# Hybrid decoder trunk: the order of work around gated linear attention (branch C)

## The chip, the cores and the metric

The kernel runs on one core of one Trainium2 chip. TensorE multiplies matrices into PSUM, VectorE, ScalarE and GpSimd do elementwise work, SyncE issues transfers, and each engine takes its own instructions in the order written and waits on semaphores for the others. The metric is the device time of one launch in microseconds (us), the median of the runs. Durations inside the kernel come from one profiled execution.

## The reference, cut to what matters

Two layers, each over 520 tokens (512 of a prompt, 8 of samples), model width 1024:

```python
z = rmsnorm(x) @ w_in                     # columns split among branches A, B, C and the gates
# A: latent attention (prompt, and samples against 4096 cached positions)
# B: spatial gating MLP
# C: gated linear attention, 4 heads, key width 64, value width 128
#    prompt: blockwise, a state per head carried along
S = exp(f)[..., None] * S + k[..., :, None] * v[..., None, :]   # samples: one step from a stored state
o = einsum('bhk,bhkv->bhv', q, S)
h_c = rmsnorm(o, g_gla) * silu(gg)        # one norm per head, over its 128 values
mix = sig(gate0) * (h_a @ w_pa) + sig(gate1) * (h_b @ w_pb) + sig(gate2) * (h_c @ w_pc)
x = x + mix @ w_o
x = x + (silu(gt) * up) @ w_down          # gt, up = rmsnorm(x) @ w_gu
```

All is float32. The kernel gets its precision by splitting each operand into a high and a low part and by three matmul passes for one product.

## The kernel before, in words

**Tiling.** Activations lie transposed, 128 channels on the partitions and 520 tokens along the row. A projection is a *group* named after its weight slab (`g03` is the fourth block of 128 columns of gate 0, `P02` the third block of `w_pa`, `wo0`, `gt0`, `up0`, `dn0` likewise). A group of `g` has 8 blocks of input channels, so 48 matmuls of 260 columns; a group of `P` has 4 and 24 matmuls. Its result takes a pair of PSUM banks, 260 columns in each.

**Weights.** ScalarE queues the load of a slab (`raw`), makes its high part (`wh`, L1223), and VectorE the low part (`wl`, L631). The helper `weights(i)` does this for every slab up to `i + 2` that isn't done yet, wherever it is called, on ScalarE and VectorE alike; TensorE waits for the low part before it starts a group. The high part of slab k waits until slab k - 3 was used.

**Banks.** `plan()` writes the groups in TensorE's order. `places()` gives each its banks, and `begin(g)` makes TensorE wait for the last reader of the group that held them before. Up to the end of the first gate stage the places are fixed or go round three pairs (the `narrow` groups, while bank 6 and 7 serve attention). After that they go round all four pairs by a counter, except some that are put on banks 6 and 7 whatever the counter says: `D0`, the even levels `L0`, `L2`, ..., `n2` and `nx`.

**Branch C's stretch.** It comes after the sample attention, whose last part is a loop of eight (`P1c`, four columns of `values`, `g1(c+1)`). The values come in pages from the cache. Then:
- `Vt0`, `Vt1`: values of branch C turned by TensorE, copied by ScalarE; `D0`, `D1`: products on the diagonal.
- seven rounds n of two levels each (`L2n`, `L2n+1`: matmuls of decayed queries and keys). VectorE collects levels 0 to 9 with `near(i)` (L1043) and makes the operands of later ones with `decayed` and `difference`; ScalarE does `decays` (exponents), and takes levels 10 to 13 with `far(i)` (L1471, L1473) and those that VectorE collected with `collected(p)` (L1480, eight copies).
- between the levels lie the gates and projections of branch A (`g00` to `g07`, `P00` to `P07`), as cover, and the samples' steps: `oh` (L1980, attention output), `Ks` (keys and values turned), `Vsel` (VectorE L1021: each sample's values on its own row, for a product), `Us` (L2013, the products k v), `sample_state` (VectorE L1033: new states), `os` (L2023, read out).
- `Kt`, `U`, `oc` (L2035, L2037): the prompt's states and outputs.
- the head norms: ScalarE squares (L1233), TensorE sums with ones (`no00` to `no11`, L1661), VectorE makes the variance (L647), ScalarE a first guess of the root (`rs_guess`, L1246), VectorE refines it in three steps (L650, L652, L654), then `y` (L1108, L1110), ScalarE the high part (`hi`, L1240), VectorE the low (`lo`, L638). `heads(p)` does this for one head after another, each with the same tiles `var`, `rs0`, `rs`.
- `merged(0, m)` (VectorE L918, L921) multiplies a gated projection and adds it; it frees the bank of `P0m`. `gate(0, m)` on ScalarE (L1387) makes the sigmoid and frees that of `g0m`.

GpSimd issues every second cache page, up to the last page of values, and sums four tiles at L2257; in this stretch it has nothing to do. Then follow the third gate stage (`g2`, `P2`), `wo`, SwiGLU (`gt`, `up`) and `dn`.

Of the kernel before, what the change touches and what calls it, by code (L numbers as in the profile page):

```python
# [14 lines left out]
GW, GH, GV = 512, 4, 128  # L15
# [199 lines left out]
def plan():  # L215
# [56 lines left out]
    for c in range(8):  # L272
        if c < 7:
            groups.append(f"pt{c + 1}n")
        if c == 2:
            groups.append("bb")
        lin(f"P1{c}")
        if c < 7:
            lin(f"g1{c + 1}")
# [5 lines left out]
    between = (["g01", "oh", "Ks0"], ["P00", "Us0"], ["g02", "Ks1", "os0"], ["P01", "Us1"], ["g03", "os1"], ["P02"], ["g04"])  # L285
# [10 lines left out]
    groups.append("oc1")  # L296
    lin("g06")
    groups.extend(["no00", "no01"])
    lin("P05", "g07")
    groups.extend(["no10", "no11"])  # L300
    lin("P06", "P07", "g20", "g21")
# [31 lines left out]
def places(groups, narrow):  # L333
# [5 lines left out]
    for g in groups:  # L339
# [44 lines left out]
def trunk(nc, a, known):  # L384
# [5 lines left out]
    with stack:  # L390
# [163 lines left out]
        assert cursor[0] <= after_ring + 16384  # L554
        Salls = [sb("Sall0", [128, 5, 128])]
# [63 lines left out]
        def _(dve):  # L619
# [83 lines left out]
            for l in range(DEPTH):  # L703
# [258 lines left out]
                for c in range(8):  # L962
# [27 lines left out]
                    if c < 7:  # L990
                        weights(si[f"g1{c + 1}"])
# [21 lines left out]

                def sample_keys(p):
                    dve.wait_ge(*upto(f"pe Ks{p}"))
                    if p:
                        dve.wait_ge(*upto("pe Us0"))
                    dve.tensor_copy(kvs[:, :, :].rearrange("p a b -> p (a b)"), bank(f"Ks{p}")[0:8, 0:384]).then_inc(*mark("dve_evac", f"free Ks{p}"))
                    dve.wait_ge(*upto(f"free Ks{p}"))
                    for e in range(2):  # L1020
                        ins = dve.tensor_tensor(Vsel[:, e, :, :],  # L1021
                                                kvs[:, 1 + e, :].unsqueeze(1).broadcast_to([8, 8, 128]),
                                                ident[0:8, 0:8].unsqueeze(2).broadcast_to([8, 8, 128]), ALU.mult)
                    ins.then_inc(*mark("value_ready", f"Vsel {p}"))
# [30 lines left out]
                weights(si["g00"])  # L1055
                evac("Ot", OT[:, :, :].rearrange("p a b -> p (a b)"), bank("Ot")[:, 0:256])
                for n in range(7):
# [7 lines left out]
                    if n == 0:  # L1065
                        weights(si["g01"])
                        sample_output()
                        sample_keys(0)
# [3 lines left out]
                    elif n == 2:  # L1072
                        weights(si["g02"])
                        sample_keys(1)
# [3 lines left out]
                    elif n == 4:  # L1078
                        for p in range(2):
                            ins = dve.memset(ATs[p][:, :, :, :], 0.0)  # L1080
                        ins.then_inc(*mark("value_ready", "AT empty"))
# [21 lines left out]
                def heads(p):  # L1103
                    for e in range(2):
                        rsqrt(f"no{p}{e}", GV, 1e-6)
                        y = ynext()
                        dve.wait_ge(*own())
                        dve.scalar_tensor_tensor(y[:, :], gvs[p][:, e, :], gn[:, G_GLA:G_GLA + 1], rs[:, :], ALU.mult, ALU.mult).then_inc(*mark("dve_step"))  # L1108
                        dve.wait_ge(*own())
                        dve.tensor_tensor(y[:, :], y[:, :], sgs[p][:, e, :], ALU.mult).then_inc(*mark("value_ready", f"y hc{p}{e}"))  # L1110
                        k = 2 * p + e
                        lo(f"hc{p}{e}", [(brl[2][:, k, :], y[:, :], brh[2][:, k, :])])
# [5 lines left out]
                gated(5)  # L1118
                weights(si["g07"])
                heads(1)  # L1120
# [84 lines left out]
        def _(act):  # L1205
# [62 lines left out]
            for l in range(DEPTH):  # L1268
# [226 lines left out]
                def heads(p):  # L1495
                    act.wait_ge(*own())
                    for e in range(2):
                        square(gvs[p][:, e, :])
                    for e in range(2):
                        rs_guess(f"no{p}{e}")  # L1500
# [5 lines left out]

                for p in range(2):
                    act.wait_ge(*upto(f"pe Vt{p}"))
                    act.activation(Vts[p][:, :, :, :].rearrange("p (a c) v w -> p a (c v w)", a=2), pair(f"Vt{p}", 512), ACT.Copy).then_inc(*mark("act_evac", f"free Vt{p}"))
                gate(0, 0)  # L1510
                for n in range(7):
                    for i in (2 * n + 7, 2 * n + 8):
                        if i < 18:
                            decays(i)
                    if n == 0:
                        gate(0, 1)
                        act.wait_ge(*upto("ha back"))
                        hi("ysm", [(brh[0][:, :, TP:T], ysm[:, :, :])], ["free oh"])
                    elif n == 1:
                        weights(si["P00"])  # L1520
                    elif n == 2:
                        gate(0, 2)
                        sample_read(0)
                    elif n == 3:
                        weights(si["P01"])
                    elif n == 4:
                        gate(0, 3)
                        sample_read(1)
                        for p in range(2):
                            collected(p)  # L1530
                    elif n == 5:
                        weights(si["P02"])
                        far(10)
                        far(11)
                    else:
# [9 lines left out]
                heads(0)  # L1545
                weights(si["P05"])
                gate(0, 7)
                heads(1)
                weights(si["P06"])
                weights(si["P07"])  # L1550
# [59 lines left out]
        def _(pe):  # L1610
# [75 lines left out]
            for l in range(DEPTH):  # L1686
# [260 lines left out]
                for c in range(8):  # L1947
# [14 lines left out]
                    values(4 * c + 3)  # L1962
                    if c < 7:
                        linear(f"g1{c + 1}", [f"g1{c + 1}"], hh, hl)

# [89 lines left out]
                gate(0, 0)  # L2055
# [5 lines left out]
                for n in range(7):  # L2061
                    level(2 * n)
                    level(2 * n + 1)
                    if n == 0:
                        gate(0, 1)
                        sample_output()
                        sample_keys(0)
                    elif n == 1:
                        branch(0, 0)
                        sample_update(0)  # L2070
                    elif n == 2:
                        gate(0, 2)
                        sample_keys(1)
# [172 lines left out]
        def _(pool):  # L2246
            S.enter(-1)
            pool.wait_ge(*upto("pages clamped"))
            for l in range(DEPTH):
# [22 lines left out]
                for i in range(16):  # L2272
                    numbers = page_numbers(mybir.EngineType.Pool, 2 * i + 1)
                    for q in range(2):
                        u = 4 * i + 2 * q + 1
                        pool.wait_ge(*upto({1: "read K61", 3: "read K63", 5: "read K63"}[u] if u < V_SLOTS else f"read V{u - V_SLOTS}"))
                        for bj in range(4):
                            pool.dma_start(vpg[u % V_SLOTS][:, bj, :],  # L2278
                                           a["cache_vals"][bass.ds(l, 1), bass.ds(numbers[4 * q + bj], 1), :, :].rearrange("a n p r -> p (a n r)")).then_inc(
                                *mark(f"values_too_loaded{u % V_SLOTS}", f"values {u}" if bj == 3 else None, 16))  # L2280
                pool.wait_ge(*upto("values 63"))
# [45 lines left out]
```

## Time and profile before

| | |
|---|---|
| median of 3 runs | 2383.04 us (2380.48 to 2391.21) |
| profiled execution | 2377.89 us, of it span 2376.2 us |
| TensorE busy | 2165.9 us, 91% of the span |
| VectorE, ScalarE, GpSimd busy | 1009.1, 721.8, 284.0 us |
| mean granted clock of TensorE | 0.958 of full speed |
| stretch from the last values to the first `oc`, layer 1 | 529.5 to 634.46 us |
| from there to `g20`, layer 1 | 634.46 to 691.35 us |
| the same in layer 2 | 1695.3 to 1802.2, and to 1859.1 us |

Times inside are from the start of the span. In a row of the timeline the first number is the start, the second how long the merged instructions took, and the bracket how long the engine had been idle and what ended it.

### The profile page before, as it was taken

The page shows a single profiled execution, that of the slowest core. Times are in us where ns is not written, and L with a number is a line of the kernel's source. Part 1 is how long each engine was busy: PE and PEld are TensorE (multiplying, and loading weights), DVE is VectorE, ACT ScalarE, POOL GpSimd, SP SyncE. Part 2 cuts the span into 40 slices and gives each one's busy share as a digit, 9 for nine tenths or more (in the row PEclk, how much of TensorE's full clock was granted, in tenths as well). Part 3 has the DMA queues.
Part 4 walks back from the last instruction along what each step waited for, and adds up shares of the span by engine and source line. Part 5 has one row for each costly group of instructions (what it writes and reads, how often), then busy time and mean ns, then how long its engine had stood idle before and what let it go on. Part 6 is the DMA issues. An engine that isn't in the chain of part 4 may idle for free.

```text
span 2376.2 us, 56296 instructions
## 1 busy us (share of the span) xinstructions
PE 2165.9 (91%) x24272; PEld 2042.0 (86%) x24272; DVE 1009.1 (42%) x1553; ACT 721.8 (30%) x1103; POOL 284.0 (12%) x522
## 2 busy tenths in 40 slices
PE   5997998988879999999979979999888899999997
PEld 5896887768869999999978878877777899999997
DVE  3566221236354544442255662222354455444323
ACT  3344113123333322222134521231333333222221
POOL 0000343540000000000000014445200000000000
PEclk8998999998989999999989989999979999999999
DMA  4212897992123232222242239889711332232221
GB/s 170 81 57 86 273 294 246 314 318 85 48 94 101 82 98 90 93 92 89 66 161 65 68 124 296 290 259 333 241 59 52 108 98 89 90 97 91 88 95 68
DMA packets 164894, 329.55 MB, mean 139 GB/s; under 512 B 24371, under 2 KB 102502, under 8 KB 163494
## 3 DMA queue, kind: packets, MB, share of 16 engines
q10 hardware_dynamic: 47520, 149.97, 19.4%
q1 hardware_dynamic: 92550, 104.64, 13.4%
q0 software_dynamic: 24576, 71.34, 9.2%
q8 instruction: 192, 3.15, 0.5%
q14 instruction: 56, 0.46, 0.1%
HBM read 311.68 MB, written 14.17 MB: 137 GB/s over the span
## 4 chain that ended last, share of the span: by engine, by line
PE 78%; DVE 8%; DMA 6%; ACT 3%; issue 3%; SPq 1%; ACTq 0%; POOL 0%; POOLq 0%; DVEq 0%; PEldq 0%
PE PS L1624 23%; PE PS L1626 21%; PE PS L1625 21%; DMA vpg<-in_cache_vals 3%; PE PS L1847 2%; DMA kpg<-in_cache_keys 2%; PE PS L1876 2%; PE PS L1675 2%; PE PS L1851 1%; DVE wl L631 1%; PE PS L1661 1%; DVE yr L672 1%; ACT wh L1223 1%; PE PS L2023 1%; PE PS L1995 1%
## 5 line engine op out<-in xcount | busy, mean ns | idle before, releaser
L1624 PE MATMUL PS<-hh,wh 128*128 128x260 f32 x3072 | 895.4, 291 | 54.6 <-DVE hl L638 26.7
L1626 PE MATMUL PS<-hl,wh 128*128 128x260 f32 x3072 | 875.5, 285 | 0.0
L1625 PE MATMUL PS<-hh,wl 128*128 128x260 f32 x3072 | 875.1, 285 | 0.0
L1624 PEld LDWEIGHTS PS<-hh,wh 128*128 128x128 f32 x3072 | 587.2, 191 | 70.5 <-issue 48.6
L631 DVE TENSOR_TENSOR wl<-raw,wh 128x1024 fp32r<-128x1024 f32 (+3 forms) x330 | 356.3, 1080 | 584.5 <-ACT wh L1223 584.1
L1625 PEld LDWEIGHTS PS<-hh,wl 128*128 128x128 f32 x3072 | 587.3, 191 | 0.2
L1626 PEld LDWEIGHTS PS<-hl,wh 128*128 128x128 f32 x3072 | 587.4, 191 | 0.0
L1223 ACT ACTIVATE wh<-raw 128x1024 fp32r<-128x1024 f32 (+3 forms) x330 | 309.4, 940 | 463.4 <-PE PS L1626 456.8
L1624 PE MATMUL PS<-fh,wh 128*128 128x260 f32 x704 | 199.1, 283 | 1.7 <-DVE yr L1177 1.7
L1626 PE MATMUL PS<-fl,wh 128*128 128x260 f32 x704 | 198.7, 282 | 0.0
L1625 PE MATMUL PS<-fh,wl 128*128 128x260 f32 x704 | 198.6, 282 | 0.0
L2269 POOL DMA_DIRECT2D kpg<-in_cache_keys x256 | 138.1, 540 | 368.9 <-PE PS L1851 209.6
L2278 POOL DMA_DIRECT2D vpg<-in_cache_vals x256 | 137.3, 537 | 132.2 <-PE PS L1876 79.4
L1624 PEld LDWEIGHTS PS<-fh,wh 128*128 128x128 f32 x704 | 132.5, 188 | 2.1 <-DVE yr L1177 2.1
L1625 PEld LDWEIGHTS PS<-fh,wl 128*128 128x128 f32 x704 | 132.5, 188 | 0.0
L1626 PEld LDWEIGHTS PS<-fl,wh 128*128 128x128 f32 x704 | 132.5, 188 | 0.0
L2257 POOL TENSOR_TENSOR sq<-xT 128x520 f32<-128x520 f32 x2 | 2.6, 1296 | 874.2 <-ACT xT L1337 874.2
L1387 ACT ACTIVATE gsig<-PS 128x520 f32<-128x520 f32 x48 | 29.0, 605 | 223.5 <-PE PS L1626 223.4
L1876 PE MATMUL PS<-vpg,pT 128*32 128x256 f32 x1024 | 71.9, 405 | 23.6 <-DMA vpg<-in_cache_vals 23.3
L1169 DVE TENSOR_TENSOR fsig<-PS,rs 128x520 f32<-128x520 f32 x44 | 30.8, 700 | 135.5 <-PE PS L1626 135.2
L1847 PE MATMUL PS<-kpg,qlz 128*32 128x128 f32 x2048 | 84.2, 279 | 4.4 <-DMA kpg<-in_cache_keys 4.2
L1591 ACT ACTIVATE fsig<-fsig 128x520 f32<-128x520 f32 x44 | 28.1, 640 | 196.2 <-DVE fsig L1169 196.2
(298 smaller groups left out, 3033.2 us busy)
## 6 DMA issues: line engine op xcount, KB each, us to landing
raw<-in_wpack ACTq DMA_DIRECT2D x242, 512.0 KB, 3.4
kpg<-in_cache_keys SPq DMA_DIRECT2D x256, 144.0 KB, 3.9
kpg<-in_cache_keys POOLq DMA_DIRECT2D x256, 144.0 KB, 3.9
vpg<-in_cache_vals SPq DMA_DIRECT2D x256, 128.0 KB, 4.1
vpg<-in_cache_vals POOLq DMA_DIRECT2D x256, 128.0 KB, 4.6
raw<-in_wpack ACTq DMA_DIRECT2D x48, 256.0 KB, 2.7
raw<-in_wpack ACTq DMA_DIRECT2D x16, 384.0 KB, 3.0
x_keep<-xT SPq DMA_DIRECT2D x2, 2080.0 KB, 14.6
```

The source lines that it names most:

```text
L631: dve.tensor_tensor(wl[s][:, 0:n], raw[s][:, 0:n], wh[k % W_RING][:, 0:n].bitcast(F32), ALU.subtract).then_inc(*mark("w_low_ready", f"wlo ...
L1169: dve.tensor_tensor(halves(fsig[f % 2][:, :]), pair(f"gt{f}"), halves(rs[:, :]), ALU.mult).then_inc(*mark("gate_scaled", f"scaled {f}"))
L1223: act.activation(wh[k % W_RING][:, 0:n], raw[k % RAW_RING][:, 0:n], ACT.Copy).then_inc(*mark("w_high_ready", f"whi {k}"))
L1387: act.activation(halves(gsig[m % 2][:, :]), pair(f"g{j}{m}"), ACT.Sigmoid).then_inc(*mark("act_evac", f"sig {j}{m}"))
L1624: pe.matmul(out, w[0], x[0], start=first, stop=False)
L1625: pe.matmul(out, w[1], x[0], start=False, stop=False)
L1626: return pe.matmul(out, w[0], x[1], start=False, stop=last)
L1675: return pe.transpose(out, in_, ident[0:n, 0:n])
L1847: ins = pe.matmul(out[32 * bj:32 * bj + 32, :], qlz[:, kk, 4 * g + bj, :], kpg[u % K_SLOTS][:, bj, PAGE * kk:PAGE * kk + PAGE], start=(g, ...
L1876: ins = pe.matmul(bank("O")[r, 256 * g:256 * g + 256], pT[c % 2][:, col % 4, r], vpg[u % V_SLOTS][:, bj, :], start=False, stop=u == 63)
L2269: pool.dma_start(kpg[u % K_SLOTS][:, bj, :], a["cache_keys"][bass.ds(l, 1), bass.ds(numbers[4 * q + bj], 1), :, :].rearrange("a n p c -> p ...
L2278: pool.dma_start(vpg[u % V_SLOTS][:, bj, :], a["cache_vals"][bass.ds(l, 1), bass.ds(numbers[4 * q + bj], 1), :, :].rearrange("a n p r -> p ...
```

## The change: what it does

- **Banks.** After the narrow groups each group gets the pair of banks that was used longest ago (`used[b]`), and only `n1`, `nx` and `D0` keep banks 6 and 7. The levels and `n2` take part like the rest.
- **First gate.** `g00` moves on all engines from behind `D1` to between the last two columns of the values, and becomes a narrow group; ScalarE takes its sigmoid before it copies `Vt`.
- **Rounds.** `Ot` stands directly behind `D1`. In round 0 `oh` and `Ks0` come before `g01`; in round 2 `Ks1` comes before `g02`.
- **Samples.** The copy of `Ks` goes from VectorE to ScalarE; `Vsel` and the clearing of the tiles `AT` go from VectorE to GpSimd, behind its last page.
- **ScalarE.** It calls `weights` at the head of each round, and does `collected` after round 6 instead of in round 4.
- **Head norms.** The chains of two heads run side by side, in tiles of their own (`hv`, `hr`) and in place. TensorE's sums `no00`, `no01` come before `oc1`, and `no10`, `no11` before `P05`. VectorE's parts are cut up: variances, roots, outputs and low parts, with weights and `merged(0, 5)` between; ScalarE's likewise: squares, guesses, high parts, with `head_high(0)` ahead of `gate(0, 6)`. Each root step still has one instruction per head, three in place of three.

```diff
@@ places
+    used = [-1] * 8
-        elif g in ("n1", "n2", "nx", "D0") or (g[0] == "L" and int(g[1:]) % 2 == 0):
+        elif g in ("n1", "nx", "D0"):
             banks = [6, 7]
...
         else:
-            banks = [2 * turn, 2 * turn + 1]
-            turn = (turn + 1) % 4
+            oldest = min(range(0, 8, 2), key=lambda b: max(used[b:b + 2]))
+            banks = [oldest, oldest + 1]
         at[g] = banks[0]
+        for b in [6, 7] if g in narrow else banks:
+            used[b] = n
+        for b in banks:
+            used[b] = n
@@ plan
-    groups.extend(["Vt0", "Vt1", "D0", "D1"])
-    lin("g00")
-    groups.append("Ot")
-    between = (["g01", "oh", "Ks0"], ["P00", "Us0"], ["g02", "Ks1", "os0"], ...
+    groups.extend(["Vt0", "Vt1", "D0", "D1", "Ot"])
+    between = (["oh", "Ks0", "g01"], ["P00", "Us0"], ["Ks1", "g02", "os0"], ...
@@ VectorE
+                weights(si["g05"])
+                gated(4)
+                head_variances(0)
+                weights(si["g06"])
+                head_roots(0)
+                ys = [head_output(0, e) for e in range(2)]
+                for e in range(2):
+                    head_low(0, e, ys[e])
+                weights(si["P05"])
+                head_variances(1)
+                merged(0, 5)
+                weights(si["g07"])
+                head_roots(1)
+                ys = [head_output(1, 0)]
+                weights(si["P06"])
+                ys.append(head_output(1, 1))
+                for e in range(2):
+                    head_low(1, e, ys[e])
                 gated(6)
                 gated(7)
@@ ScalarE
+                for p in range(2):
+                    collected(p)
                 weights(si["P03"])
                 gate(0, 5)
                 outputs(0)
+                head_squares(0)
                 weights(si["P04"])
+                head_guesses(0)
                 outputs(1)
+                head_squares(1)
+                weights(si["g06"])
+                head_high(0)
                 gate(0, 6)
-                heads(0)
                 weights(si["P05"])
+                head_guesses(1)
                 gate(0, 7)
-                heads(1)
                 weights(si["P06"])
+                head_high(1)
@@ TensorE
                 outputs(0)
                 branch(0, 4)
+                sums("no00", 1)
+                sums("no01", 1)
                 outputs(1)
                 gate(0, 6)
-                sums("no00", 1)
-                sums("no01", 1)
+                sums("no10", 1)
+                sums("no11", 1)
                 branch(0, 5)
                 gate(0, 7)
-                sums("no10", 1)
-                sums("no11", 1)
@@ GpSimd
+                for p in range(2):
+                    pool.wait_ge(*upto(f"free Ks{p}"))
+                    if p:
+                        pool.wait_ge(*upto("pe Us0"))
+                    for e in range(2):
+                        ins = pool.tensor_tensor(Vsel[:, e, :, :], kvs[...] (8x8x128, broadcast), ident[...], ALU.mult)
+                    ins.then_inc(*mark("sample_values", f"Vsel {p}"))
+                pool.wait_ge(*upto("pe Us1"))
+                for p in range(2):
+                    ins = pool.memset(ATs[p][:, :, :, :], 0.0)
```

## Rows read from the trace of the kernel before

**Rows 1.** The page: the chain that ended last, by engine.
```profile
PE 78%; DVE 8%; DMA 6%; ACT 3%; issue 3%; SPq 1%; ACTq 0%; POOL 0%; POOLq 0%; DVEq 0%; PEldq 0%
```

**Rows 2.** TensorE's waits: us in total, times, longest.
```profile
PE PS L1624 <- DVE gtmp L918: 2.7, 2, 1.3
...
PE PS L1624 <- DVE yr L1177: 1.7, 2, 0.9
PE PS L1624 <- DVE xT L1151: 1.6, 2, 0.8
```

**Rows 3.** TensorE's timeline of layer 1, rows with a wait.
```profile
531.96 0.64 PE L1876 MATMUL PS<-vpg,pT 128*32 128x256 f32 x8 [1.38 <-DMA vpg<-in_cache_vals]
534.74 0.93 PE L1876 MATMUL PS<-vpg,pT 128*32 128x256 f32 x8 [2.14 <-DMA vpg<-in_cache_vals]
540.18 0.76 PE L2053 MATMUL PS<-gq,gk 64*32 64x32 f32 x64 [0.59 <-DVE ATd L1053]
562.28 0.56 PE L1624 MATMUL PS<-hah,wh 128*128 128x260 f32 x1 [2.76 <-issue]
590.10 1.55 PE L1995 MATMUL PS<-zz 64*32 64x32 f32 x128 [3.24 <-DVE S L1033]
608.19 0.65 PE L1997 MATMUL PS<-zz 64*32 64x32 f32 x32 [6.33 <-ACT AT L1471]
622.20 0.98 PE L1675 MATMUL PS<-ident,zz 128*128 128x128 f32 x7 [1.17 <-ACT AT L1473]
655.61 1.99 PE L1661 MATMUL PS<-sq,ones 128*128 128x260 f32 x8 [1.46 <-ACT sq L1233]
674.35 3.81 PE L1661 MATMUL PS<-sq,ones 128*128 128x260 f32 x8 [8.10 <-ACT sq L1233]
691.35 0.56 PE L1624 MATMUL PS<-hh,wh 128*128 128x260 f32 x1 [7.30 <-DVE wl L631]
```

**Rows 4.** Windows: from:to, length, busy (instructions), granted clock, DMA share, GB/s.
```profile
529.50:634.46 104.96, 87.34 (x1458) 0.87 0.27 86
634.46:691.35 56.89, 40.04 (x266) 0.92 0.19 67
1695.30:1802.20 106.90, 90.12 (x1457) 0.84 0.25 81
1802.20:1859.10 56.90, 39.88 (x266) 0.91 0.20 70
```

**Rows 5.** Windows of `P00` and `P02` after a wait, `g05`, `oc0`, `P04`.
```profile
562.28:566.85 4.57, 4.57 (x24) 0.63 0.06 10
608.77:613.93 5.16, 5.16 (x31) 0.55 0.01 3
...
628.61:634.46 5.85, 5.85 (x50) 1.00 0.14 48
634.46:639.80 5.34, 5.34 (x31) 1.00 0.00 0
639.80:642.79 2.99, 2.99 (x26) 1.00 0.32 93
```

**Rows 6.** VectorE's timeline.
```profile
559.48 2.35 DVE L1021 TENSOR_TENSOR Vsel<-kvs,ident 8x1024 f32<-8x1024 f32 x2
...
587.90 2.15 DVE L1033 SCALAR_TENSOR_TENSOR S<-S,efs,PS 128x128 f32<-128x128 f32 x8
...
658.90 0.70 DVE L652 SCALAR_TENSOR_TENSOR rs<-rs,var 128x520 f32<-128x520 f32 x1
```

**Rows 7.** ScalarE's timeline: table load, sigmoid, high part of a slab.
```profile
553.42 1.28 ACT L1387 ACT_TABLE_LOAD   x1
554.71 0.60 ACT L1387 ACTIVATE gsig<-PS 128x520 f32<-128x520 f32 x1
...
649.21 1.06 ACT L1223 ACTIVATE wh<-raw 128x1024 fp32r<-128x1024 f32 x1
```

**Rows 8.** GpSimd's groups, forms apart: count, busy us, mean ns.
```profile
L2257 POOL TENSOR_TENSOR sq<-xT 128x520 f32<-128x520 f32 x2 | 2.6, 1296 | 874.2 <-ACT xT L1337 874.2
```

More of the change, by code:

```diff
@@ L277, in plan @@
         lin(f"P1{c}")
-        if c < 7:
-            lin(f"g1{c + 1}")
+        lin(f"g1{c + 1}" if c < 7 else "g00")
     narrow.update(groups[wide:])
-    groups.extend(["Vt0", "Vt1", "D0", "D1"])
-    lin("g00")
-    groups.append("Ot")
-    between = (["g01", "oh", "Ks0"], ["P00", "Us0"], ["g02", "Ks1", "os0"], ["P01", "Us1"], ["g03", "os1"], ["P02"], ["g04"])
+    groups.extend(["Vt0", "Vt1", "D0", "D1", "Ot"])
+    between = (["oh", "Ks0", "g01"], ["P00", "Us0"], ["Ks1", "g02", "os0"], ["P01", "Us1"], ["g03", "os1"], ["P02"], ["g04"])
     for n, names in enumerate(between):
@@ L295, in plan @@
     lin("P04")
-    groups.append("oc1")
+    groups.extend(["no00", "no01", "oc1"])
     lin("g06")
-    groups.extend(["no00", "no01"])
-    lin("P05", "g07")
     groups.extend(["no10", "no11"])
-    lin("P06", "P07", "g20", "g21")
+    lin("P05", "g07", "P06", "P07", "g20", "g21")
     for m in range(8):
@@ L338, in places @@
     at, before, held, turn = {}, {}, {}, 0
-    for g in groups:
+    used = [-1] * 8
+    for n, g in enumerate(groups):
         if prompt_banks(g):
@@ L989, in _ @@
                     merged(1, c)
-                    if c < 7:
-                        weights(si[f"g1{c + 1}"])
+                    weights(si[f"g1{c + 1}" if c < 7 else "g00"])
                 dve.wait_ge(*upto("exps 7"))
@@ L1012, in sample_output @@
                     lo("ysm", [(brl[0][:, :, TP:T], ysm[:, :, :], brh[0][:, :, TP:T])])
[L1014 to L1024, printed above, removed]
                 def sample_state(p):
@@ L1101, in _, with head_variances @@
                     ins.then_inc(*mark("dve_evac", f"free U{p}"))
-                def heads(p):
+                def head_variances(p):
                     for e in range(2):
[L1105 to L1112, printed above, removed]
+                        dve.wait_ge(*upto(f"pe no{p}{e}"))
+                        dve.tensor_scalar(halves(hv[e][:, :]), pair(f"no{p}{e}"), 1.0 / GV, 1e-6, ALU.mult, ALU.add).then_inc(*mark("var_ready", f"free no{p}{e}"))
@@ L1493, in outputs, with head_squares @@
                     ins.then_inc(*mark("act_evac", f"free oc{p}"))
-                def heads(p):
+                def head_squares(p):
                     act.wait_ge(*own())
@@ L1498, in heads, with head_guesses, head_high @@
                         square(gvs[p][:, e, :])
+                def head_guesses(p):
                     for e in range(2):
-                        rs_guess(f"no{p}{e}")
+                        act.wait_ge(*upto(f"free no{p}{e}"))
+                        act.activation(hr[e][:, :], hv[e][:, :], ACT.Abs_reciprocal_sqrt).then_inc(*mark("rs0_ready", f"rs0 no{p}{e}"))
+                def head_high(p):
+                    for e in range(2):
                         y = ynext()
@@ L1505, in heads, with sample_keys @@
                         hi(f"hc{p}{e}", [(brh[2][:, 2 * p + e, :], y[:, :])], [f"y hc{p}{e}"])
+                def sample_keys(p):
+                    act.wait_ge(*upto(f"pe Ks{p}"))
+                    if p:
+                        act.wait_ge(*upto("pe Us0"))
+                    act.activation(kvs[:, :, :].rearrange("p a b -> p (a b)"), bank(f"Ks{p}")[0:8, 0:384], ACT.Copy).then_inc(*mark("act_evac", f"free Ks{p}"))
+                gate(0, 0)
                 for p in range(2):
@@ L1509, in _ @@
                     act.activation(Vts[p][:, :, :, :].rearrange("p (a c) v w -> p a (c v w)", a=2), pair(f"Vt{p}", 512), ACT.Copy).then_inc(*mark("act_evac", f"free Vt{p}"))
-                gate(0, 0)
                 for n in range(7):
+                    weights(si[("g01", "P00", "g02", "P01", "g03", "P02", "g04")[n]])
                     for i in (2 * n + 7, 2 * n + 8):
@@ L1528, in _ @@
                         sample_read(1)
-                        for p in range(2):
-                            collected(p)
                     elif n == 5:
-                        weights(si["P02"])
                         far(10)
                         far(11)
-                    else:
+                    elif n == 6:
                         gate(0, 4)
@@ L2054, in _ @@
                     ins.then_inc(*mark("group_ready", f"pe D{p}"))
-                gate(0, 0)
                 begin("Ot")
```

57 lines of the change are left out of this document (39 added, 18 removed).

## The prediction

> **What bounds the kernel now.** I read the page first, for the chain that ended last: 78% of it is TensorE itself [rows 1]. So only what makes TensorE idle, or run slowly, can be had; no matmul is taken away. Next TensorE's waits, and then its timeline through branch C, where the reader is to see ten waits in 160 us [rows 3]: 1.38 + 2.14 for pages, 0.59, 2.76, 3.24, 6.33 and 1.17 among the levels, 1.46, 8.10 and 7.30 in the head norms. That is 17.6 us before `oc0` and 16.9 us after it. The windows show both layers alike: 104.96 and 106.90 us up to `oc0`, 56.89 and 56.90 us from there to `g20` [rows 4]. Last the clock: behind a wait part of the time is at 1.2 instead of 2.4 GHz (0.63 and 0.55 of full speed on average), so `P00` took 4.57 and `P02` 5.16 us where `P04` took 2.99 [rows 5].
>
> **Why TensorE waits there.** The code gives the cause of each wait.
> - 2.76: `P00` has banks 6 and 7, after `L2`, whose `near(2)` VectorE does only behind `Vsel`, 2.35 us [rows 6].
> - 3.24: `L8` is put on 6 and 7, where the counter had also put `Us1`, and waits for eight state updates, 2.15 us [rows 6].
> - 6.33: `L11` gets 6 and 7 directly after `L10`; ScalarE reads `L10` only after eight copies (`collected`), a table load, an exponent and a slab.
> - 8.10: `no10` waits for squares that ScalarE does after both heads of `heads(0)`, each a serial chain with VectorE. 7.30: `g20` waits for its low part, which VectorE makes after `heads(1)`.
>
> **The change part by part, one layer.** I went through the new order with the old durations: a `g` group 5.85 us, a `P` group 2.99, an `oc` 5.34 [rows 5].
>
> *Values and first gate.* `g00` now stands ahead of the last column, and its 5.85 us are longer than the two waits for pages, so these 3.52 us go. `g00` needs a slab that is ready and a bank read long ago, so the move costs nothing. `D1` no longer shares banks with `D0`: 0.59 goes. `Vt0` is copied after the sigmoid, and `Ot` needs its bank; by my count it is free about 1 us ahead.
>
> *Levels.* I worked the banks out by the new rule. `P00` gets the pair of `Ks0`, which ScalarE has copied: 2.76 goes. `L8` gets that of `L6`: 3.24 goes. `L11` gets that of `L9`: 6.33 goes, since `far(10)` now comes before `collected`. The copies of `collected` then have two groups of cover ahead of `oc0`. `Kt1` takes the pair of `L12`, which ScalarE reads after `gate(0, 4)`; so of 1.17 about 0.7 stays.
>
> One wait is new. `g02` gets the pair of `Us0`, that is, it waits for `sample_state(0)`. Between `Us0` and `g02` there are only `L4`, `L5` and `Ks1`, about 1.7 us; VectorE has to finish a slab and `merged(0, 0)` (three operations of 0.7) and then needs 2.15 us [rows 6]. I get 1.3 us of wait. Bounds: 0, if VectorE is 1.3 us early, and 3, if it starts the round late.
>
> *Clock here.* `P00`, `P02`, `g03` and the `Vt` are slow behind waits that go; against the same groups at full clock that is 1.6 and 2.2 [rows 5], and about 2.4 for the other two and the last page. Against it, `Vt`, `D`, `Ot`, two levels, `oh` and `Ks0` now stand in one run of some 10 us of small matmuls with no gate among them. The trace doesn't show such a run; near it the clock did fall, as with `P00`. I take 2.5 us, from 0 to 5.
>
> Sum before `oc0`: 17.6 - 0.7 - 1.3 + 6.2 - 2.5 = 19.3 us gained.
>
> *Vsel and clearing on GpSimd.* The trace shows GpSimd in a two-input operation of 520 elements at 1.30 us [rows 8]. By elements 1024 take 2.55, two of them 5.1 us. `Ks0` is copied about 1.2 us after `g01` starts, and `g01`, two levels and `P00` (10.1 us) stand ahead of `Us0`; so `Vsel` is ready 10.1 - 1.2 - 5.1 = 3.8 us before it is needed, and `Vsel` 1 likewise. GpSimd has issued its last page by then, so nothing is queued behind it. The memset isn't in the trace at this size; it has 13 us before `far(10)`, over twice what the same row gives, 5.1. Both at nothing; upper end, if such an operation takes twice as long, 1 to 2 us in each of two places.
>
> A rule of the Trainium skill speaks against this part: in "SBUF — State Buffer", section "SBUF: two separate sides", an operation of VectorE with two inputs in SBUF and one of GpSimd that reads SBUF can't run together; the later one is held up for the whole of the other. No row of this trace has the two together on branch C.
>
> *Head norms.* TensorE from the start of `oc0`, with nothing to wait for: 2 x 5.34 (`oc`), 2 x 5.85 (`g06`, `g07`), 4 x 2.99 (`P04` to `P07`), 4 x 0.82 (sums; the pair took 1.64 from 655.61 to the next group's start) = 37.6 us instead of 56.9. The squares for `no00` are ready at 6.6 + 0.6, ahead of 8.3; the 1.46 goes, and with `heads` cut up the 8.10 too.
>
> But one wait is new, and it is the largest. VectorE's `weights(g06)` wants slab 70 (`g07`), whose high part ScalarE makes after `outputs(1)` and two squares. `oc1` ends at 15.3; copies and squares to 17.6, the slab 1.06 [rows 7] to 18.7, the low part to 19.9. Only then come six root operations at 0.73 (0.70 [rows 6] and a step between) to 24.3, two outputs of two operations each to 25.8 and 27.3. ScalarE's `head_high(0)` follows these and ends at 28.1. `gate(0, 6)` stands behind it, with a table load of 1.28 and the sigmoid of 0.60 [rows 7]: 30.0. By the rule of age `g07` gets the pair of `g06` and so waits for this sigmoid, while TensorE is ready at 25.8. That is 4.3 us, and the clock behind it 1.6 as at `P00`. After that nothing is late: VectorE's second chain ends at 45, `g20`'s slab is ready at 42.1 and TensorE comes at 43.5. Gain: 56.9 - 43.5 = 13.4. `g20` and `g21` after the 7.30 took 13.4 together instead of 11.7, so another 1.7 comes back.
>
> *Behind branch C.* `wo0` waited for `P27` (`gtmp`), `gt0` for `wo7` (`xT`), `dn0` for `up21` (`yr`): 2.7 + 1.6 + 1.7 in both layers [rows 2]. By age the first gets the pair of `P26`, the second that of `P27`, the third that of `up20`; all of it goes, 6.0 us. `up1` now waits for `gt0`, read 7 us before. The rest of the kernel keeps its banks.
>
> **Sum.** Two layers: 2 x (19.3 + 13.4 + 1.7) + 6.0 = 74.8 us. From the profiled execution's own 2377.9 (span 2376.2 and 1.7 around it): 2303 us, 3.15% less. Against the median of 2383.0, which is 0.2% above that execution, 2308 us. 0.5%, or 12 us, is what a measurement can tell from no change.
>
> **The rivals.**
> - *The wait at `g07` is hidden* (chance 0.12). If VectorE gets through its chain 4.3 us sooner than I count, 2 x 5.9 us more are gained: 2296. For it: the order was cut fine enough to give every other group its cover. Against it: each step has a row.
> - *New waits take the place of the old ones* (0.19). The three engines are now interleaved so that each hands over within a few us; a round that starts late costs `g02`, `Kt1`, `g07` and `g20` together. If half of what branch C gives comes back, 0.5 x 68.8 = 34 us: 2342. For it: five of the ten waits [rows 3] were of this kind. Against it: VectorE and ScalarE have idle time in each round.
> - *VectorE and GpSimd block each other* (0.07). If `Vsel` falls on VectorE's `decayed`, one product of 2.55 us delays `sample_state` or the levels, twice in a layer: 4 x 2.55 = 10 us, 2318. For it: eight of VectorE's operations in a round read two tiles of SBUF. Against it: by my count VectorE waits for the next level during both. The rule of the Trainium skill named above would bring this about.
> - *No change* (0.03). If TensorE's waits merely move, 2383. Against it: the 8.10 and 7.30 come of orders that are gone.
> - *Slower* (0.02): GpSimd's products. TensorE is in order and `Us` waits for `Vsel`. With two products of t us at each of four places, less the 5.1 + 3.8 that are covered, the gain is eaten up at 4 x (2t - 8.9) = 74.8, t = 13.8 us; at 16 us the kernel is 18 us slower, 2401. Nothing is near this: the row has 1.30 for half the elements [rows 8].
>
> **How the numbers follow.** The forecast has the remaining 0.57, with 2308. Its own range comes from the bounds: `g02` 0 to 3, the run of small matmuls 0 to 5, GpSimd up to 4, all twice: 2298 to 2325. The range reaches to both neighbours, 2292 to 2342. Faster by over 0.5% 0.95, less some doubt about waits I didn't see: 0.94; within 0.5% 0.04; slower 0.02.
>
> **What the profile after would show.** No wait of TensorE on L1876 in the last column, none on `near` before `P00`, none at `L8` or `L11`; about 1.3 us at `g02` on L1033 and 4 us at `g07` on the sigmoid; the window from `oc0` to `g20` 43 to 44 us; `Vsel` on GpSimd at about 2.5 us each; no wait at `wo0`, `gt0`, `dn0`. The prediction is wrong if `g07` doesn't wait, if `Us` waits for GpSimd, or if the clock stays low over the run up to `Ks0`.

## The result, and the profile after

The changed kernel took 2314.03 us (median of 4 runs, 2310.12 to 2317.98) beside 2387.12 us for the kernel before on the same chip: ratio 0.9693, 95% interval 0.9654 to 0.9732. The forecast was 2308 us, a ratio of 0.9685. The profiled execution took 2310.12 us, of it a span of 2308.4, which is 67.8 us less than the span before.

The page of the kernel after, engines and chain of work (before: [rows 1]):

```profile
PE 2158.6 (94%) x24272; PEld 2037.8 (88%) x24272; DVE 989.6 (43%) x1537; ACT 722.9 (31%) x1107; POOL 303.9 (13%) x534
...
PE 80%; DVE 6%; DMA 6%; issue 3%; ACT 3%; SPq 1%; ACTq 0%; POOLq 0%; POOL 0%; DVEq 0%; PEldq 0%
```

TensorE does the same work in nearly the same busy time (2158.6 us, before 2165.9); what went is mostly idle time. The windows of the kernel after, cut at the same instructions as [rows 4] (last values to `oc0`, `oc0` to `g20`, both layers; each engine's busy time follows the length, then granted clock, DMA share and GB/s):

```profile
527.98:616.93 88.95, 85.91 (x1458) 79.07 (x1457) 50.02 (x117) 39.32 (x60) 10.12 (x6) 0.92 0.33 101
616.93:659.40 42.47, 39.43 (x268) 35.86 (x267) 24.75 (x37) 20.42 (x29) 0.00 (x0) 0.96 0.16 45
1660.55:1754.44 93.89, 89.41 (x1457) 82.52 (x1457) 49.22 (x115) 39.42 (x60) 10.12 (x6) 0.87 0.30 93
1754.44:1796.86 42.42, 39.37 (x267) 35.80 (x266) 24.70 (x37) 20.37 (x29) 0.00 (x0) 0.96 0.16 44
```

Against [rows 4] that is 16.0 and 13.0 us less before `oc0`, and 14.4 and 14.5 less behind it. `g20` and `g21` together took 11.7 in both layers instead of 13.4 and 13.5: 3.5 more. The three waits of [rows 2] are gone: 6.0. Together 67.4 of the span's 67.8. Outside these stretches the two executions still differ: 1.5 us less ahead of layer 1's stretch, 1.9 more between the layers, 0.8 less at the end, which nearly cancel.

TensorE's waits in the kernel after, those of branch C (us in total, times, longest):

```profile
PE PS L1653 <- ACT gsig L1401: 6.1, 2, 3.0
...
PE PS L2027 <- issue: 4.1, 2, 2.7
...
PE PS L1653 <- DVE S L1023: 2.0, 2, 1.0
...
PE PS L1704 <- ACT AT L1487: 1.5, 2, 0.7
```

And where they stand in layer 1, TensorE's timeline of the kernel after (before: ten waits, [rows 3]):

```profile
541.12 1.05 PE L2027 MATMUL PS<-zz 64*32 64x32 f32 x96 [1.33 <-issue]
...
564.07 0.39 PE L1653 MATMUL PS<-hh,wh 128*128 128x260 f32 x1 [0.97 <-DVE S L1023]
...
604.99 0.66 PE L1704 MATMUL PS<-ident,zz 128*128 128x128 f32 x4 [0.73 <-ACT AT L1487]
...
646.06 0.39 PE L1653 MATMUL PS<-hh,wh 128*128 128x260 f32 x1 [3.04 <-ACT gsig L1401]
```

Four instead of ten. Three were forecast: `g02` behind `sample_state(0)` (1.3 forecast, 0.97 here), `Kt1` (0.7, 0.73) and `g07` behind the sigmoid of `gate(0, 6)` (4.3, 3.04). The first was not: an idle time in the middle of `L0`. This level is 64 matmuls in a row with no semaphore between them (a row of the timeline can merge it with `L1`, 64 more). 32 ran, then TensorE stood for 1.33 us, then the rest ran. In layer 2 it stood for 2.73, behind 60:

```profile
1672.00 0.72 PE L2027 MATMUL PS<-zz 64*32 64x32 f32 x60
1675.46 1.00 PE L2027 MATMUL PS<-zz 64*32 64x32 f32 x68 [2.73 <-issue]
```

The code has TensorE wait only ahead of a level, so no data can be late there.

### The profile page after: what moved, and what is told of

The parts are those of the page before. It is cut to its first block, busy times and chain, and to the rows that moved or that the text cites. A ratio compares the mean times of both kernels' runs of the same rounds, so it can differ in the third digit from the quotient of the medians.

```text
span 2308.4 us, 56282 instructions
## 1 busy us (share of the span) xinstructions
PE 2158.6 (94%) x24272; PEld 2037.8 (88%) x24272; DVE 989.6 (43%) x1537; ACT 722.9 (31%) x1107; POOL 303.9 (13%) x534
## 3 DMA queue, kind: packets, MB, share of 16 engines
q8 instruction: 192, 3.15, 0.6%
## 4 chain that ended last, share of the span: by engine, by line
PE 80%; DVE 6%; DMA 6%; issue 3%; ACT 3%; SPq 1%; ACTq 0%; POOLq 0%; POOL 0%; DVEq 0%; PEldq 0%
PE PS L1653 23%; PE PS L1655 22%; PE PS L1654 22%; DMA vpg<-in_cache_vals 3%; DMA kpg<-in_cache_keys 3%; PE PS L1876 2%; PE PS L1905 2%; PE PS L1704 2%; PE PS L1880 1%; PE PS L1690 1%; DVE wl L634 1%; DVE yr L675 1%; PE PS L2055 1%; ACT wh L1237 1%; SPq L2234 1%
```

## Experiments

Each kernel below was timed beside the kernel before on its own chip, and the ratio is to that one. "Head stretch" is the window from the last values to `oc0`, "tail" that from `oc0` to `g20`. Two of a kind are layers 1 and 2. Each window is from one execution, and such a stretch differs between executions with nothing changed in it: the head stretch of the old order took 104.96 and 106.90 us in the kernel before, and 102.71 and 105.08 in the kernel with new head norms alone. Where a diff shows only `plan`, the engines' own code follows the same order.

**Which part gives what: the banks alone.** The kernel before with the new rule for banks, and the old order of everything.

```diff
-        elif g in ("n1", "n2", "nx", "D0") or (g[0] == "L" and int(g[1:]) % 2 == 0):
+        elif g in ("n1", "nx", "D0"):
             banks = [6, 7]
...
-            banks = [2 * turn, 2 * turn + 1]
-            turn = (turn + 1) % 4
+            oldest = min(range(0, 8, 2), key=lambda b: max(used[b:b + 2]))
+            banks = [oldest, oldest + 1]
```

> The kernel before with the bank rule by age alone; order, head norms and Vsel as before. Theory (each wait of the stretch has its own cause in the banks): in each layer the 0.59 at D1, the 2.76 at P00 and the 3.24 at L8 go; of the 6.33 some 2.3 us stay, now at L13, because ScalarE still does collected ahead of far(10); about 1.1 us are new at g02, since VectorE still does Vsel ahead of near(2); the clock gives back 2 to 3 us. With 6.0 us behind branch C (wo0, gt0, dn0) that is about 32 us of the 67.8 that the whole change gained in its span: ratio 0.986. The window from oc0 to g20 stays at 56.9 us. Rival (the waits only move, and the order has to change with them): less than 15 us, ratio above 0.993.

Ratio 0.9867 (0.9828 to 0.9905): near the theory's 0.986, and the rival's 0.993 is outside. The parts came out otherwise than expected. TensorE's waits and the windows of layer 1 of this kernel:

```profile
PE PS L1666 <- ACT sq L1238: 19.1, 4, 8.1
PE PS L1629 <- DVE wl L636: 15.1, 4, 7.4
...
PE PS L1629 <- DVE gtmp L923: 7.5, 5, 2.5
```

```profile
534.27:629.46 95.19, 88.05 (x1458) 80.69 (x1457) 57.61 (x125) 38.64 (x58) 0.00 (x0) 0.89 0.31 95
629.46:686.36 56.90, 39.91 (x266) 35.50 (x265) 27.01 (x38) 19.65 (x28) 0.00 (x0) 0.91 0.20 69
```

The head stretch is 9.8 us shorter than in [rows 4] (in layer 2 it took 95.43 us, 11.5 shorter), the tail has not moved: 56.90, with its waits for squares and for the low part untouched. The waits of 2.76, 3.24 and 6.33 are gone, the last wholly: the 2.3 us expected at `L13` didn't come. But with the old order the rule brings waits of its own: 2.53 at `g02` for `gtmp`, the pair of `P00`, where 1.1 was expected (in layer 2 1.05 at `g02` and 1.27 at `g03`), which the change avoids by its order of `Ks1` and `g02`. The clock gave nothing back in layer 1 (88.05 us of busy time, 87.34 before), 2 to 3 were expected. And `wo0` still waits 1.33 for `gtmp` in both layers, so behind branch C the rule alone brings 3.3 of the 6.0.

**The head norms alone.** The kernel before with only the last part of the change: sums ahead of `oc1` and `P05`, chains side by side and cut up (the diff under "The change", from `head_variances` to `head_high`).

> The kernel before with the head norms of the changed kernel alone (order on TensorE, ScalarE and VectorE from outputs(0) on, tiles of their own); banks by the old counter. Theory: the window from oc0 to g20 goes from 56.9 to 42.4 us as in the changed kernel, with the same wait of 3.0 us at g07 (the counter gives it the pair of g06 too), and g20 and g21 start at full clock, 1.7 us more: 2 x 16.2 = 32 us, ratio 0.986. Rival (the head norms need the banks by age or the earlier collected to pay): a window above 46 us.

Ratio 0.9829 (0.9790 to 0.9868). The windows of the tail, layers 1 and 2, and two of TensorE's waits in this kernel:

```profile
623.46:665.86 42.40, 39.35 (x267) 35.78 (x266) 24.68 (x37) 20.35 (x29) 0.00 (x0) 0.96 0.15 44
1774.97:1817.36 42.39, 39.34 (x268) 35.77 (x267) 24.67 (x37) 20.35 (x29) 0.00 (x0) 0.96 0.15 44
```

```profile
PE PS L2039 <- ACT AT L1502: 12.5, 2, 6.3
PE PS L1666 <- ACT gsig L1418: 6.1, 2, 3.0
```

The tail is that of the full change within 0.1 us, its new wait at `g07` included, and the 6.33 before `L11` is still there. So the tail gains the same with either bank rule. The ratio lies below the expected 0.986, which is inside its interval; by the windows the part brings 2 x 14.5 us and 3.4 at `g20` and `g21`, 32.4 in all.

The gains of the two parts, 1.33% and 1.71%, add up to 3.04% beside 3.07% for the full change, but this leaves no room for the new place of `g00` and the order of the rounds, and each figure is uncertain by 0.4. By the windows the banks alone bring 9.8 + 11.5 + 3.3 = 24.6 us and the head norms 32.4, together 57.0 of the 67.4. The other 10.4 belong to the order: 6.2 and 1.5 in the head stretches, 2.7 at `wo0`. No run has the order alone.

**The new wait at `g07`.** The kernel after with one line moved on ScalarE.

```diff
                 weights(si["g06"])
-                head_high(0)
                 gate(0, 6)
+                head_high(0)
                 weights(si["P05"])
```

> The changed kernel with gate(0, 6) ahead of head_high(0) on ScalarE, nothing else. Theory (g07 waits for the sigmoid of g06, which stands behind the high parts of two heads): the wait of 3.04 us at g07 goes and with it 1.5 us of low clock; g20 may wait 0.4 us for its slab on VectorE. The window from oc0 to g20 goes from 42.4 to 38.1 us in both layers, 8.6 us in all: ratio about 0.966 instead of 0.9693. Rival (VectorE's chain of both heads is the bound, and the wait moves on to g20): the window stays above 41 us and the ratio at 0.969.

Ratio 0.9676 (0.9647 to 0.9706), beside 0.9693 (0.9654 to 0.9732): the intervals overlap, so what the line is worth is read from the windows. Those of the tail, and TensorE's waits for a low part (two of the four are at `g20`, 0.64 and 0.63):

```profile
611.23:649.49 38.26, 37.63 (x266) 34.09 (x265) 22.40 (x34) 19.32 (x27) 0.00 (x0) 1.00 0.17 49
...
1747.89:1786.14 38.25, 37.62 (x266) 34.09 (x265) 22.39 (x34) 19.32 (x27) 0.00 (x0) 1.00 0.17 49
```

```profile
PE PS L1653 <- DVE wl L634: 1.7, 4, 0.6
```

The wait of `g07` for `gsig` is gone, the clock stays at full speed through the tail, and 37.63 us of busy time is the 37.6 that the prediction had added up for TensorE with nothing to wait for. What the wait cost is 42.47 - 38.26 = 4.2 us in each layer: 3.0 of idle time and 1.8 of slow matmuls behind it (39.43 - 37.63), less 0.6 that `g20` now waits for its low part.

**GpSimd's part.** The kernel after, with `Vsel` and the clearing back on VectorE.

```diff
-                for p in range(2):
-                    pool.wait_ge(*upto(f"free Ks{p}"))
...
@@ VectorE, round 0 (and round 2 for Vsel 1, round 4 for the clearing)
                         sample_output()
                         weights(si["g01"])
+                        sample_values(0)
```

> The changed kernel with Vsel and the clearing of AT back on VectorE (Vsel behind sample_output and weights(g02), the clearing in round 4); the copy of Ks stays on ScalarE. Theory (with Ks0 ahead of g01 and P00 no longer behind near(2), VectorE has 6.8 us of idle time for the 2.35 of Vsel, so GpSimd buys nothing): no wait of TensorE changes by more than 0.5 us, ratio 0.969 within its interval. Rival (the move to GpSimd is what takes the 2.76 away): P00 or g02 wait 2 to 3 us more in each layer, ratio 0.971.

Ratio 0.9718 (0.9689 to 0.9747), beside 0.9693 (0.9654 to 0.9732) with GpSimd: no difference that the intervals carry. The ratio alone would sooner speak for the rival's 0.971 than for the theory's 0.969, so the trace has to decide. TensorE's waits in this kernel:

```profile
PE PS L1668 <- ACT gsig L1416: 6.1, 2, 3.1
PE PS L2042 <- issue: 4.4, 2, 3.0
...
PE PS L1719 <- ACT AT L1502: 1.5, 2, 0.7
```

The same, and nothing new at `P00`, `Us0` or `L8`; the wait at `g02` is 0.59 and 1.03, where the rival wanted 2 to 3 us more. The waits of 2.76 and 3.24 in the kernel before came of the banks: with these dealt by age VectorE has the time for `Vsel` as well. That the change moved it to GpSimd took no wait away; a gain of a few us in the time is not excluded by these intervals.

**The idle time in `L0`.** Two theories: the run from `Vt` to `Ks0` is too long a run of small matmuls, and its instructions arrive late; or the clock and TensorE are slow there for another reason, and the place of `g01` doesn't matter. First, `g01` ahead of `oh`, with `Ks0` behind `D1`; the run up to `L0` stays whole:

```diff
-    groups.extend(["Vt0", "Vt1", "D0", "D1", "Ot"])
-    between = (["oh", "Ks0", "g01"], ...
+    groups.extend(["Vt0", "Vt1", "D0", "D1", "Ks0", "Ot"])
+    between = (["g01", "oh"], ...
```

> The changed kernel with the run of small matmuls cut behind the levels: g01 again ahead of oh (as before the change), and Ks0 right behind D1, so that Vsel stays early. Theory (the unbroken run Vt, D, Ot, L0, L1, oh, Ks0 lets the clock fall): oh goes from 4.8 and 7.0 us (the two layers) to 3.6, g01 from 7.9 to 6.0; the stall without a releaser inside L0 (1.3 and 2.7 us) stays, since what stands before it is as long as it was. 6 to 8 us in all, ratio 0.966. Rival (the clock falls later by as much, or P00 now waits for VectorE): ratio 0.969.

Ratio 0.9693 (0.9662 to 0.9724), as the rival has it: no gain. The idle time in `L0` stays, 1.56 and 1.12. It now stands behind 29 and 57 matmuls of `L0` instead of 32 and 60, and the three matmuls of `Ks0` now stand ahead of `L0`: it has kept its place in the count of instructions. `oh` and `g01` ran at full clock, 3.64 and 6.0 us, but the groups behind them then didn't. Windows of this kernel: head stretch of layer 1, `oh`, `P00`, `g02`, head stretch of layer 2:

```profile
529.95:622.53 92.58, 89.11 (x1457) 82.43 (x1457) 50.77 (x117) 39.52 (x60) 9.33 (x6) 0.87 0.32 100
550.43:554.07 3.64, 3.64 (x42) 3.62 (x47) 0.00 (x0) 0.89 (x2) 0.00 (x0) 0.99 0.00 0
555.49:559.41 3.92, 3.92 (x30) 3.78 (x25) 3.82 (x10) 1.79 (x2) 0.00 (x0) 0.76 0.28 71
564.26:571.71 7.45, 7.45 (x48) 7.32 (x48) 4.61 (x11) 2.92 (x4) 2.79 (x2) 0.77 0.51 143
1666.58:1753.38 86.80, 83.83 (x1457) 77.19 (x1457) 51.08 (x117) 39.51 (x60) 9.33 (x6) 0.94 0.33 104
```

The two layers are the same program, and TensorE is busy for 89.11 us in one and 83.83 in the other. Here the granted clock differs, 0.87 and 0.94, and it isn't set by the order alone.

Then `g01` between the diagonal and `Ot`, so that it cuts the run in two:

```diff
-    groups.extend(["Vt0", "Vt1", "D0", "D1", "Ot"])
-    between = (["oh", "Ks0", "g01"], ...
+    groups.extend(["Vt0", "Vt1", "D0", "D1", "Ks0"])
+    lin("g01")
+    groups.append("Ot")
+    between = (["oh"], ...
```

> The changed kernel with g01 right behind D1 and Ks0, ahead of Ot and the levels. Theory (the stall inside L0 is TensorE's instructions arriving late: small matmuls use them up several times faster than a gate group, and a packet of the instruction queue starts just there): with a gate group in between the stall goes too; P00 may wait 0.5 us for the samples' low part. Up to 12 us in all, ratio 0.964 to 0.966. Rival (the stall is a wait on z or on a bank that the trace doesn't name): it stays at 1.3 to 2.7 us in L0.

Ratio 0.9681 (0.9650 to 0.9711), beside 0.9693 (0.9654 to 0.9732) without the cut: by the time alone this is no difference. The head stretches of this kernel, and its `P00` in layer 1:

```profile
531.46:617.01 85.55, 83.91 (x1458) 77.40 (x1458) 48.73 (x114) 36.82 (x58) 9.32 (x6) 0.94 0.32 101
...
555.24:559.60 4.36, 4.36 (x31) 4.22 (x24) 4.26 (x11) 0.64 (x1) 0.00 (x0) 0.67 0.23 64
1659.71:1747.28 87.57, 86.21 (x1458) 79.66 (x1457) 49.70 (x116) 36.94 (x58) 9.32 (x6) 0.90 0.32 100
```

No idle time without a releaser is left among the levels in either layer, and the head stretches are 3.4 and 6.3 us shorter than after the change. The expected ratio was lower still, 0.964 to 0.966; among what is missing are `P00`, which took 4.36 at 0.67 with no wait before it, and `oh` in layer 2, 4.59 instead of 3.64.

**Where `g00` stands.** The same idle time could also be met by another order: the kernel after with `g00` back behind `D1`.

```diff
-        lin(f"g1{c + 1}" if c < 7 else "g00")
+        if c < 7:
+            lin(f"g1{c + 1}")
...
-    groups.extend(["Vt0", "Vt1", "D0", "D1", "Ot"])
+    groups.extend(["Vt0", "Vt1", "D0", "D1"])
+    lin("g00")
+    groups.append("Ot")
```

> The changed kernel with g00 back behind D1 on all engines; everything else stays. Theory (moving g00 took away the waits for the last pages, but lengthened the run of small matmuls): the waits for pages in the last column come back, 1.3 to 3.5 us a layer with slow Vt behind them in the worse case, and the stall in L0 and some of the low clock go; the net is within 3 us a layer, ratio 0.968 to 0.971. Rival (the move is worth what the prediction gave it, 3.5 us and the clock, with nothing on the other side): ratio 0.9725.

Ratio 0.9725 (0.9692 to 0.9758), beside 0.9693 (0.9654 to 0.9732): the intervals overlap, and the time alone doesn't decide. The value is the rival's and lies outside the theory's 0.968 to 0.971, which the interval reaches. The head stretches took 92.21 and 92.66 us, that is 3.3 more and 1.2 less than after the change. TensorE's timeline in this kernel shows what is traded:

```profile
530.45 0.64 PE L1910 MATMUL PS<-vpg,pT 128*32 128x256 f32 x8 [3.07 <-DMA vpg<-in_cache_vals]
...
1659.93 0.64 PE L1910 MATMUL PS<-vpg,pT 128*32 128x256 f32 x8 [2.57 <-DMA vpg<-in_cache_vals]
...
1665.97 0.24 PE L2087 MATMUL PS<-gq,gk 64*32 64x32 f32 x5 [1.13 <-issue]
```

The waits for the last page are back, and with them slow `Vt` (3.40 and 3.08 instead of 1.97); `wo0` waits for `gtmp` again, 1.33 us in both layers, as the deal of the banks is shifted by one group. `L0` has no gap, and in layer 2 the idle time without a releaser has moved into `D1`, behind 47 of its 64 matmuls. There, behind the same 47, it also stood in the kernel before, 2.10 us in layer 2, and with the banks alone, 2.95. The kernel with the head norms alone has this order too, but longer waits for the last pages (2.03 and 1.21), and no such idle time. So it is no matter of one group.

**Both amendments together:** `g01` behind the diagonal, and `gate(0, 6)` ahead of `head_high(0)`.

> The order of split together with gate(0, 6) ahead of head_high(0). Theory (the two act in separate stretches, so their gains add): 8.6 us for the gate and up to 12 for the cut run from the changed kernel's time, ratio 0.961 to 0.963. Rival (one hides the other): not below 0.965.

Ratio 0.9630 (0.9601 to 0.9659), 2293.21 us beside 2380.14, as expected: the fastest of all, though its interval still touches that of the changed kernel. The windows say more; head stretches and tails are 20.2 us shorter than after the change. They are:

```profile
529.59:615.12 85.53, 83.97 (x1457) 77.46 (x1457) 48.62 (x114) 36.83 (x58) 9.33 (x6) 0.94 0.32 100
615.12:653.38 38.26, 37.63 (x267) 34.09 (x265) 22.40 (x34) 19.32 (x27) 0.00 (x0) 1.00 0.16 49
1656.52:1742.05 85.53, 83.82 (x1458) 77.29 (x1458) 49.57 (x116) 36.95 (x58) 9.34 (x6) 0.94 0.32 102
1742.05:1780.29 38.24, 37.62 (x266) 34.08 (x265) 22.38 (x34) 19.32 (x27) 0.00 (x0) 1.00 0.16 49
```

## Why the prediction was right

The likeliest case came true: every wait that was to go went, and the three new ones stand where they were forecast. That 2308 us comes so near is in part luck. The parts were forecast at 74.8 us and brought 67.4 in the traces, 3.3 and 6.3 too little before `oc0` and 1.0 and 1.1 more than forecast behind it; the medians happen to lie 73.1 apart. By its own steps:

- **Waits before `oc0`.** Idle time there is length less TensorE's busy time: 17.62 and 16.78 in [rows 4], 3.04 and 4.48 after. So 14.6 and 12.3 went, where 17.6 - 0.7 - 1.3 = 15.6 was forecast. What is missing is the unforeseen idle time in `L0`, 1.33 and 2.73. The run of small matmuls was priced by the clock alone, not by a stop.
- **Clock before `oc0`.** This is the term that was mis-sized: 6.2 - 2.5 = 3.7 forecast, and busy time fell by 1.4 and 0.7. Part of the 6.2 did come: `P00` took 3.15 instead of 4.64 in layer 1 and `Vt` 1.97 instead of 3.30. But `P02`, down for 2.2 because it stood behind the 6.33, still took 4.88 with no wait before it, at a clock of 0.60 in the row below. And the run cost more than its upper bound of 5 in layer 2: `oh` took 6.99 instead of 3.64 and `g01` 7.96 instead of 6.0, 5.3 together, and the 2.73 in `L0` on top (in layer 1 4.75 and 7.93, 3.0 together). The sign "the clock stays low over the run up to `Ks0`" came in part: `Vt`, `D` and `Ot` ran at full clock, but `oh` and `Ks0`, the last two groups of the run, didn't: 0.75 over both in layer 1, 0.50 over `oh` in layer 2, behind the idle time of 2.73. Windows of the kernel after: `P00` and `P02` in layer 1, `oh` in layer 2:

```profile
556.32:559.40 3.08, 3.08 (x32) 2.95 (x25) 2.90 (x9) 1.86 (x2) 0.00 (x0) 1.00 0.27 82
591.92:596.73 4.81, 4.81 (x32) 4.67 (x25) 1.68 (x3) 3.18 (x6) 0.00 (x0) 0.60 0.23 58
1676.39:1683.30 6.91, 6.91 (x40) 6.91 (x34) 3.29 (x9) 1.26 (x2) 0.00 (x0) 0.50 0.01 2
```

- **Tail.** 43.5 forecast, 42.4 measured. The 37.6 of work and the 1.6 of clock were right (37.6 and 1.8), the wait at `g07` was 1.3 too long. VectorE and ScalarE of the kernel after, ahead of that wait:

```profile
636.87 0.69 DVE L1095 SCALAR_TENSOR_TENSOR var<-var,rs 128x520 f32<-128x520 f32 x1
637.48 0.69 DVE L1095 SCALAR_TENSOR_TENSOR hv<-hv,hr 128x520 f32<-128x520 f32 x1
638.09 0.69 DVE L1098 TENSOR_TENSOR var<-var,rs 128x520 f32<-128x520 f32 x1
...
643.46 0.64 ACT L1254 ACTIVATE hch<-yr 128x520 fp32r<-128x520 f32 x1 [0.68 <-DVE yr L1111]
644.11 1.28 ACT L1401 ACT_TABLE_LOAD   x1
645.41 0.60 ACT L1401 ACTIVATE gsig<-PS 128x520 f32<-128x520 f32 x1
```

  The chain is the one forecast, link by link: roots, outputs, `head_high(0)`, table load, sigmoid. But two heads side by side start a root step every 0.61 us, where one head's chain before went at 0.73 (658.17, 658.90, 659.64). Six steps at 0.73 instead of 0.61 are 0.7 of the 1.3. The outputs and the high parts came some 0.2 sooner, and TensorE came to `g07` 0.3 later than forecast, 26.1 us behind the start of `oc0` instead of 25.8.
- **`g20`, `g21`, `wo0`, `gt0`, `dn0`.** 1.7 twice and 6.0 forecast, 3.5 and 6.0 measured.
- **`Vsel` on GpSimd.** 5.1 us for two products forecast, 4.53 or 3.74 measured, ready at 552.6, long before `Us0` at 559.4. Nothing waits for it. The experiment says more than the prediction did: on VectorE it would have made TensorE wait no longer either.
- **Layer 2.** The prediction doubled layer 1. In layer 2 of the kernel before there was one page wait of 1.33 in this window, not 3.52, and the 2.10 in `D1`, which the prediction left out. The layers' idle times differ by 0.8 in [rows 4], so little was lost by it, but the 2.10 was the warning for `L0`.
- **The range.** The forecast's own lower end doesn't follow from its bounds: 2 x (1.3 + 2.5) = 7.6 us below 2308 is 2300, not 2298. And 2292 lies 4 us beyond the neighbour at 2296.

The rival "the wait at `g07` is hidden" needed 4.3 us from VectorE's chain; it got 1.3. "New waits take the place of the old ones" had its mechanism, but beside the waits forecast only the 4.1 in `L0`, and `g20` waited for nothing. "VectorE and GpSimd block each other" is real (see the last section), but in the changed kernel only GpSimd was held up, 4.53 instead of 3.74 us, with time to spare.

**What stays open.** Why the clock falls where it does. The head stretch with the same TensorE order took 85.91 and 89.41 us of busy time in the kernel after, 84.21 and 89.51 with `gate(0, 6)` moved, 89.63 and 87.64 with `Vsel` on VectorE; with the run cut in two it took 83.91, 86.21, 83.97 and 83.82. On average that is 87.7 against 84.5, which suggests that the cut helps the clock too, but one layer and the next differ by up to 5.3 with nothing changed. That the idle time in `L0` and `D1` is instructions that arrive late is well supported, but no run isolates it. No semaphore can hold a matmul within a group. In all four kernels with the run whole, the idle time stands behind the same matmul, counted from the gate ahead of the last values: the 194th in layer 1 and the 222nd in layer 2, with 16 of the values, 16 of `Vt`, 128 of `D`, 2 of `Ot` and, in one kernel, 3 of `Ks0` ahead of those of `L0`. And in the traces a packet of 0.02 MB on instruction queue q8 starts 2.2 to 2.6 us before TensorE goes on, in all eleven cases: 538.86 and 541.12 in layer 1 of the kernel after, 1673.26 and 1675.46 in layer 2. With the head norms alone this packet starts at 1678.11, some 2.4 us before the 47th matmul of `D1`, and there TensorE doesn't stop. A gate of 48 long matmuls in between makes the idle time vanish. No run changed the number of instructions alone.

## What to carry to other kernels

Where an engine in order has several kinds of cover, deal PSUM banks by age before you move work to another engine: here it removed the waits of 2.76 and 3.24 us that the move was to help with, though with the old order it brought one of 2.53. When a table load and a sigmoid free the banks that TensorE waits for, put them ahead of work that itself waits for a chain: one line moved was 4.2 us of the window in each layer. And when small matmuls are gathered, cut the run with one long group (3.4 and 6.3 us here), and look at the last groups' granted clock and not at waits alone.

## What the runs showed of the hardware

- **VectorE and GpSimd block each other in SBUF, for whole instructions.** In the kernel with `g01` ahead of `oh`, VectorE's and GpSimd's timelines:

```profile
542.12 3.75 POOL L2317 TENSOR_TENSOR Vsel<-kvs,ident 8x1024 f32<-8x1024 f32 x2 [13.07 <-ACT kvs L1531]
...
544.12 1.03 DVE L1033 COPY_PREDICATED ATd<-lev,PS 128x256 f32<-128x256 int32 x2 [1.92 <-PE PS L2027]
545.04 1.11 DVE L958 TENSOR_TENSOR zz<-gk,dd 128x256 f32<-128x256 f32 x1
546.07 0.41 DVE L959 TENSOR_TENSOR zz<-gq,dd 128x256 f32<-128x256 f32 x1
```

  L958, a product of two tiles in SBUF, takes 0.42 us elsewhere and 1.11 here: it ends 0.28 behind GpSimd's pair (545.87). In layer 2 the same instruction took 1.42 and ended 0.28 behind the pair as well. The copies on L1033, which read PSUM, were not held up. The other way round, `Vsel` took 4.53 where VectorE's `wl` (raw and `wh`, both in SBUF, 1.22 us) was under way when it started, and 3.74 where not. This is the rule of the Trainium skill, "SBUF — State Buffer", section "SBUF: two separate sides", that was weighed ahead of the change, and here the trace agrees with it. In this kernel no wait of TensorE comes of it: VectorE is idle again before its next level.
- **An idle time without a releaser inside a group of small matmuls**, 1.1 to 3.5 us. It stands in `L0` in both layers of the four kernels that have the run from the last values to `L1` whole, and in neither layer of the two in which `g01` cuts it. With `g00` behind `D1` it stands in `D1`, in layer 2 of three kernels out of four. Each time an instruction packet on q8 starts 2.2 to 2.6 us before it ends.
- **Independent VectorE instructions of 520 columns start every 0.61 us, dependent ones every 0.73**: the root steps of two heads in turn (636.87, 637.48, 638.09) and of one head (658.17, 658.90, 659.64 in the kernel before).
- **The granted clock falls without a wait.** `P02` ran at 0.60 of full speed in the kernel after (between the levels 1.2 and 2.4 GHz) behind groups that ran back to back. TensorE had not waited since 564.07 and ran at full clock up to 586.78; then `os1`, 32 matmuls of one column, ran at 0.77 and the level pair behind it at 0.50.
